# Encoder trunk on one core: expert weights stored one block per ring unit, recurrence products in halved columns, first turn started on half of the keys and values

## What is computed

```python
def wkv_scan(r, w, k, v, a, b, reverse):            # both directions, 16 heads
    def step(state, inp):
        r_t, w_t, k_t, v_t, a_t, b_t = inp
        sa = jnp.einsum('bhvk,bhk->bhv', state, a_t)
        state = state * w_t[:, :, None, :] + sa[..., None] * b_t[:, :, None, :] + v_t[..., None] * k_t[:, :, None, :]
        return state, jnp.einsum('bhvk,bhk->bhv', state, r_t)

def moe_swiglu(h, router, w13, w2):                  # 8 experts, hidden width 3584
    for e in range(N_EXPERTS):
        out = out + combine[:, e:e + 1] * swiglu(t, w13[e], w2[e])
```

## Time and profile before

| | us |
|---|---|
| median of 3 runs (2158.40 to 2160.73) | 2159.16 |
| profiled execution, its own time | 2160.95 |
| its span | 2159.1 |

### The profile page before, as it was taken

The page is one execution under the profiler, slowest core; times in us unless marked ns, Lnnn a source line. Parts: engine busy times, 40 slices in busy tenths (PEclk is TensorE's granted clock), DMA queues, the critical chain, the costliest instruction groups (busy, mean ns, idle before and its releaser), DMA issues.

```text
span 2159.1 us, 56930 instructions
## 1 busy us (share of the span) xinstructions
PE 1936.5 (90%) x26300; PEld 1585.1 (73%) x26300; DVE 511.1 (24%) x1305; ACT 261.7 (12%) x558; POOL 192.5 (9%) x318
## 2 busy tenths in 40 slices
PE   8999988999979899999789888988888888888887
PEld 4454455877635588888588887888888888888876
DVE  2132131000171546552411112011120111201200
ACT  2121121000002244332000000000000000000000
POOL 1111111000011336421000000000000000000000
PEclk9999999999989899999899999999999999999999
DMA  9432433545321011002799999999999999999992
GB/s 360 150 123 79 155 117 122 170 156 164 123 78 35 8 21 26 18 12 100 233 355 347 354 335 303 350 349 346 348 302 345 347 346 338 348 330 328 342 330 86
DMA packets 352750, 473.86 MB, mean 219 GB/s; under 512 B 30104, under 2 KB 288432, under 8 KB 352512
## 3 DMA queue, kind: packets, MB, share of 16 engines
q1 hardware_dynamic: 349632, 460.05, 63.3%
q0 software_dynamic: 2080, 7.37, 1.0%
q10 hardware_dynamic: 800, 2.76, 0.3%
HBM read 460.04 MB, written 10.10 MB: 218 GB/s over the span
## 4 chain that ended last, share of the span: by engine, by line
PE 85%; issue 7%; DVE 5%; ACT 2%; DMA 1%; POOL 1%; SPq 0%; DVEq 0%; POOLq 0%
PE ps L692 29%; PE ps L1270 14%; PE ps L683 14%; PE ps L806 12%; PE ps L744 7%; PE ps L757 3%; PE ps L860 1%; PE ps L967 1%; PE ps L773 1%; DVE arena L1874 1%; PE ps L1200 1%; DVE arena L1876 1%; PE ps L1207 0%; PE ps L791 0%; DMA arena<-wqkv 0%
## 5 line engine op out<-in xcount | busy, mean ns | idle before, releaser
L692 PE MATMUL ps<-arena 128*64 128x96 f32 x14336 | 636.5, 247 | 87.0 <-issue 86.1
L692 PEld LDWEIGHTS ps<-arena 128*64 128x64 f32 x14336 | 611.5, 137 | 107.0 <-issue 106.9
L683 PE MATMUL ps<-arena 128*128 128x128 f32 (+11 forms) x2498 | 382.4, 327 | 34.5 <-DVE arena L1861 8.3
L683 PEld LDWEIGHTS ps<-arena 128*128 128x128 f32 (+3 forms) x2498 | 297.5, 191 | 116.1 <-issue 59.2
L1270 PE MATMUL ps<-arena 128*64 128x96 f32 x7168 | 320.4, 245 | 51.7 <-issue 51.7
L1270 PEld LDWEIGHTS ps<-arena 128*64 128x64 f32 x7168 | 305.3, 136 | 61.5 <-issue 61.5
L806 PE MATMUL ps<-arena 128*128 128x512 f32 x576 | 253.4, 596 | 1.9 <-DMA arena<-wqkv 1.9
L2137 DVE TENSOR_TENSOR arena<-arena,ps 128x192 f32<-128x192 f32 x112 | 39.7, 355 | 788.9 <-ACT arena L1567 788.8
L806 PEld LDWEIGHTS ps<-arena 128*128 128x128 f32 x576 | 108.1, 191 | 128.7 <-issue 125.9
L744 PE MATMUL ps<-arena 128*128 128x256 f32 x704 | 153.8, 381 | 0.0
L744 PEld LDWEIGHTS ps<-arena 128*128 128x128 f32 x704 | 134.5, 191 | 20.2 <-issue 1.9
(11 more groups left out here) (246 smaller groups left out, 979.9 us busy)
## 6 DMA issues: line engine op xcount, KB each, us to landing
arena<-mw SPq DMA_DIRECT2D x336, 1024.0 KB, 7.9
arena<-wqkv SPq DMA_DIRECT2D x36, 1024.0 KB, 7.4
arena<-fw SPq DMA_DIRECT2D x32, 1024.0 KB, 6.4
arena<-wrkv SPq DMA_DIRECT2D x12, 1024.0 KB, 7.3
arena<-awo SPq DMA_DIRECT2D x4, 1024.0 KB, 6.2
arena<-bwo SPq DMA_DIRECT2D x4, 1024.0 KB, 11.9
xg<-arena POOLq DMA_DIRECT2D x8, 384.0 KB, 9.2
arena<-xg SPq DMA_DIRECT2D x7, 384.0 KB, 10.3
```

Source lines behind the costliest of these rows:

```text
L683: last = mm(o, a, b, start=(n == 0), stop=(n == len(pairs) - 1))
L692: last = mm(o[c], a[:, c], b, start=(n == 0), stop=(n == len(pairs) - 1))
```

## The change

Four parts.

1. The host stores w13 and w2 so that each unit is one block [128 partitions, 4096 floats]; a new `tiled_unit` loads it as two DMAs, each taking 8 KB from each of 128 rows of 16 KB. What lies in the ring slot is the same as before.
2. `add_y`, the products of `values`, and the 64-wide steps of the chain with all rows (z1 to z4 of the early half) are done in two 64-column halves, as the experts' are.
3. The first turn: DVE and POOL wait for copy 6 of `rkv_sb` in place of 8, with later waits where the other half is read (turn 2 for k, copy 10 or 12 for v); project(8) and (9) move behind the operands and systems; `inverse_rows(0, 1, 16)` and `inverse_out(0)` come before all four `pairings_out(0, i)`.
4. In the other turns inverse rows 14 and 15 and `inverse_out` move behind the copy of y and two `pairings_out`. POOL starts d_b only when the first mix is done.

```diff
             def expert_unit(item, i):
                 e, kind, n, u = item
-                w13 = mw13[bass.ds(i * 2 + e, 1)].rearrange("e (k p) n -> p (e k) n", p=P)
-                wd = mw2[bass.ds(i * 2 + e, 1)].rearrange("e (k p) n -> p (e k) n", p=P)
-                c = n * 256
-                if kind == "up":
-                    ff_unit(kind, u, (w13[:, :, c:c + 256], w13[:, :, FFE + c:FFE + c + 256]), None, FFE)
-                else:
-                    ff_unit(kind, u, None, wd[:, 4 * n:4 * n + 4, :], FFE)
+                tiled_unit(u, (mw13 if kind == "up" else mw2)[bass.ds(i * 2 + e, 1), n])
+            def tiled_unit(u, w):
+                w, half = w.rearrange("o p n -> p (o n)"), SLOT // 2
+                halves(u, (unit(u)[:, 0:half], unit(u)[:, half:]), (w[:, 0:half], w[:, half:]))
...
             def add_y(t, h, lhsT, rhs, first=False, last=False):
-                c = t * RQ + h * RH
-                return mm(ps[:, 4, c:c + RH], lhsT, rhs, start=first, stop=last, skip_group_check=True)
+                at = t * RQ + h * RH
+                for c in COLS:
+                    ins = mm(ps[c, 4, at:at + RH], lhsT[:, c], rhs, start=first, stop=last, skip_group_check=True)
+                return ins
...
-                    last = run(ps[:, 7, c:c + RH], [(gm23[i % 2][0][:, h, :], value(q, t, h))])
+                    last = by_halves(ps[:, 7, c:c + RH], [(gm23[i % 2][0][:, h, :], value(q, t, h))])
...
-                        last = run(ps[rows, bank, h * width:(h + 1) * width], [(of[:, h, rows], by[:, h, :])])
+                        o = ps[rows, bank, h * width:(h + 1) * width]
+                        product = by_halves if width == RH and rows == slice(0, P) else run
+                        last = product(o, [(of[:, h, rows], by[:, h, :])])
...
             project(7)
-            project(8)
-            project(9)
             operands(0, 0)
             operands(0, 1)
             system(0, 0)
             system(0, 1)
-            project(10)
+            project(8)
             operands(0, 2)
             operands(0, 3)
             system(0, 2)
             system(0, 3)
+            project(9)
+            project(10)
             project(11)
...
-            dve.wait_ge(rkv_sb, 8)
+            dve.wait_ge(rkv_sb, 6)
...
                 if nq:
-                    inverse_rows(nq, 11, BLK)
-                    inverse_out(nq)
+                    inverse_rows(nq, 11, 14)
                 dve.wait_ge(Y.ps, q + 1)
                 dve.wait_ge(head_done, q + 1)
                 dve.tensor_copy(y_sum.rearrange("p t n -> p (t n)"), ps[:, 4, :]).then_inc(Y.sb, 1)
                 if nq:
-                    for i in range(4):
-                        pairings_out(nq, i)
+                    pairings_out(nq, 0)
+                    pairings_out(nq, 1)
+                    inverse_rows(nq, 14, BLK)
+                    inverse_out(nq)
+                    pairings_out(nq, 2)
+                    pairings_out(nq, 3)
...
-            pairings_out(0, 0)
-            pairings_out(0, 1)
-            inverse_rows(0, 1, 7)
-            pairings_out(0, 2)
-            inverse_rows(0, 7, 12)
-            pairings_out(0, 3)
-            inverse_rows(0, 12, BLK)
+            inverse_rows(0, 1, BLK)
             inverse_out(0)
+            for i in range(4):
+                pairings_out(0, i)
...
             pool.wait_ge(rms_h, H_DONE[2])
+            pool.wait_ge(mix_ready, KB)
             pool.tensor_tensor(d_b[:, :, 0:S - 1], hR[:, :, 1:S], hR[:, :, 0:S - 1], ALU.subtract).then_inc(db_ready, 1)
...
-            pool.wait_ge(rkv_sb, 8)
+            pool.wait_ge(rkv_sb, 6)
...
+                if q == 2:
+                    pool.wait_ge(rkv_sb, 8)
...
-                if q == 0:
-                    pool.wait_ge(rkv_sb, 12)
+                pool.wait_ge(rkv_sb, 10 + 2 * (q // 2))
...
+        "mw13": a["m_w13"][0].reshape(EXPERTS, KB, P, 2, GE, 256).transpose(0, 4, 2, 1, 3, 5).reshape(EXPERTS, GE, P, SLOT),
+        "mw2": a["m_w2"][0].reshape(EXPERTS, GE // 2, 4, P, D).transpose(0, 1, 3, 2, 4).reshape(EXPERTS, GE // 2, P, SLOT),
```

More of the change, by code:

```diff
@@ L656, in _ @@
                     e = sp.value_load(over_i[0:1, bass.ds(j + (OVER + 1), 1)], min_val=0, max_val=EXPERTS - 1)
-                    w13 = mw13[bass.ds(e, 1)].rearrange("e (k p) n -> p (e k) n", p=P)
-                    wd = mw2[bass.ds(e, 1)].rearrange("e (k p) n -> p (e k) n", p=P)
                     sp.wait_ge(down_ps, j * (GE // 2) + EXPERTS * GE // 2)
@@ L665, in _ @@
                             sp.wait_ge(s, j * per + (EXPERTS * per + c))
[L666 to L670, removed]
+                        tiled_unit(u, (mw13 if kind == "up" else mw2)[bass.ds(e, 1), n])
             sp.wait_ge(experts_done, 1)
@@ L1531, in _ @@
             project_out(7)
-            project_out(8)
-            project_out(9)
             for i in (0, 1):
@@ L1537, in _ @@
                 system_out(0, i)
-            project_out(10)
+            project_out(8)
             for i in (2, 3):
@@ L1542, in _ @@
                 system_out(0, i)
-            project_out(11)
+            for c in (9, 10, 11):
+                project_out(c)
             late_keys(0, 0)
@@ L1810, in key_rates @@
                         dve.wait_ge(bonus_ok, q)
+                        dve.wait_ge(rkv_sb, 12)
                 dve.wait_ge(za.sb, q * 4 + 2 * d + 2)
@@ L2415 @@
         "g2": a["b_g2"][0], "bwo": a["b_wo"][0], "fw13": a["f_w13"][0], "fw2": a["f_w2"][0],
-        "router": a["m_router"][0], "mw13": a["m_w13"][0], "mw2": a["m_w2"][0],
+        "router": a["m_router"][0],
+        "mw13": a["m_w13"][0].reshape(EXPERTS, KB, P, 2, GE, 256).transpose(0, 4, 2, 1, 3, 5).reshape(EXPERTS, GE, P, SLOT),
+        "mw2": a["m_w2"][0].reshape(EXPERTS, GE // 2, 4, P, D).transpose(0, 1, 3, 2, 4).reshape(EXPERTS, GE // 2, P, SLOT),
     }
```

## The result

The changed kernel takes 2098.92 us (median of 4, 2084.22 to 2105.03), the kernel before 2158.78 beside it. The ratio is 0.971 (95% interval 0.966 to 0.977): 60 us faster, where 183 were forecast. Its profiled execution took 2093.34, with a span of 2091.4.

The account below looks back on a forecast made before the run. Instruction refills queued behind weight transfers were taken to bound the experts. From the profiled 2160.95 us, 137 for the experts and 46 for the recurrence came off: 1978, or 1976 as a median, range 1946 to 2014 (chance 0.58).

Parts of the forecast that it names:

- Bounds: Experts: PE's gaps are instruction refills queued behind weights until the unit in front drains; some 0.95 us a unit, gapless unit 5.36.
- Layout, the rate: Experts' weight loads: 8 KB runs move a unit in 5.05 us, the 4 KB runs' rate, against 5.71 on the mix.
- Layout, "if all of it comes off a gap": Experts: a refill waits 0.66 us less; if all comes off the 0.95 us gap, the period falls from 6.31 to about 5.65.
- queues that run empty: Experts: shorter transfers empty the queue once a unit, more refills wait only 1.6 us; period taken as 5.5, 5.36 if all do.
- Phase: Experts: part 2's 5.5 added instruction blocks move cuts half a unit, near a unit's start; most positions there give 5.4 to 5.6.
- the opposite: Experts, rival (c), slower: refills line up right behind the unit just issued, 7.2 us a unit, experts 1152, time 2193; chance 0.10.
- Rival (a): Experts: transfers gain only half as much, or refills stay in mid-load; period 6.0, experts 1018, time 2059; chance 0.17.
- Halved products: Recurrence: 64-column halves save 1.9 (early chain), 0.8 (early sums) and 3.1 us (values, add_y) a turn; last turn 4.3.
- End of a turn: Recurrence: the 2.77 us stall for masked pairings goes, 5.8 with the halved values; GT late costs 0.5 us a turn.
- First turn: Recurrence, first turn: pairings start at about 727.5 in place of 735.55, chain about 15 us later; 19 gained, bounds 11 and 21.
- "issue" below 25 us: Sign in the experts: L692's idle time released by "issue", 86.1 us before, would fall below 25.
- the first q8 packet at 1.6 us: Sign in the experts: the first instruction-refill packet after a gap comes at 1.6 us, not 4.5.

Follow-up runs that it names:

- tiny_loads: Changed kernel; from the third expert on each of a unit's two DMAs brings 64 of 2048 elements a row; sixth expert: PE busy for all of 110.9 us.
- layout_only: Kernel before with the new weight layout alone, cuts staying in mid-unit: 2120.88 us, ratio 0.981, experts 1028.2 us against 1072.0.
- pad32_7of8: Changed kernel plus 32 tiny products, weight DMAs bringing 1792 of 2048 elements from the third expert on: experts 3 to 8 749.9 us, against 763.5 with full transfers.
- first_turn_only: Kernel before with part 3 (the first turn) alone: first copy of y at 798.1 us against 816.4, experts start at 1055.2 against 1070.6.

## Why the prediction was wrong

Two steps of the sum for the experts failed: that all of the saved transfer comes off a gap, and that the move of the cuts does no harm. The recurrence came out at the forecast total, in part by luck.

**Bounds (right, with one size wrong).** Gaps are refills behind weights: shown by `tiny_loads`. A gapless unit was taken as 5.36 us; with hardly any weights it is 5.28. But a refill doesn't wait until the unit in front has drained: about 1.4 of its 2.1 MB pass first.

**Layout, the rate (right).** Up units reach the rate of the 4 KB runs. 6.03 and 5.08 came from good windows: by the share of q1 from 1100 to 1900 us, a unit held the engines for 6.22 us before (267.48 MB at 99.2%) and 5.55 after (263.45 MB at 87.2%). Both are half a microsecond longer than I took, but the difference is the 0.66 of the sum. Queue q1 in that window, before and after:

```profile
q1 hardware_dynamic: 199091, 267.48, 99.2%
...
q1 hardware_dynamic: 36525, 263.45, 87.2%
```

**Layout, "if all of it comes off a gap" (the first step that failed).** The layout gave, at one position, 44, 30 and 59 us over 168 units: 0.26, 0.18 and 0.35 us a unit (0.21, 0.21 and 0.37 by the medians), about half of the 0.66 or less. I had all of it, and another 0.15 on top for queues that run empty. Nor did the waits shrink by it: from the kernel before to `layout_only` the median wait of a refill goes from 3.8 to 3.6 us only, while the gaps become fewer (154 to 112) and shorter (1.01 to 0.77 us in the median). My explanation, not shown by a run of its own: the wait is the end of the traffic in front less the time of the request, and when the period shrinks, the next unit is issued earlier too, so that a part of what the transfer saves is taken back. It agrees in sign with `pad32_7of8`.

**Phase (seen, and taken on the wrong side: the second step that failed).** The move by half a unit was right to the record. I wrote that most positions near a unit's start give 5.4 to 5.6 and one side the opposite, and gave the opposite 0.10. The changed kernel landed on that opposite side for six of its eight experts: 1050 where the new layout in mid-unit has 1028 and 1019. My price for it, 1152, was far too high: a gap is 1 us a unit, and not one long block in two, because the refill waits for about as long as in mid-unit (medians 4.0 us, and 3.8 in the kernel before). And the good positions, -1 to -32, lie 24 records away and give 964 to 977; the forecast's 935 was reached nowhere with all weights moving. Position was the term that decided, worth 86 us against 44 for the layout. It ought to have been a case with a chance for each side, worked out from where SP's issue stands to the cut, and not part of the sum.

**Rival (a)** named half of the transfer's gain, 1018 us for the experts: it is near what the new layout gives in mid-unit (1028, 1019). For the changed kernel it is 32 too few. The Trainium skill (Runtime: NRT & Kernel Launch, Instruction fetch mechanics) calls the crossing of a block "mostly hidden". That holds where hardly any weights move (110.8 us of PE in 110.8) and for 60 us of the changed kernel's seventh expert, and fails by about 1 us a block elsewhere. The rule of the Trainium skill that a DMA engine turns between its rings packet by packet (DMA: Bandwidth & Descriptors, Queues, rings and completion order) is not tested by these runs: a packet there is a group of descriptors (about 9 to 17), while a packet of the profile is one run of up to 8 KB here (263.45 MB in 36525 packets after the change). Ahead of a refill pass 11 of the profile's packets on each of the 16 engines after the change and 74 before it (medians), and 1.4 MB in both. So the forecast's sentence that the rule would have a refill wait for one packet, against 4.5 us, compared two different things.

**Halved products (each turn within 3 us of its size).** By halves alone a turn was to give 5.8 and its last 4.3. They gave 4.5, 5.1 and 7.3. Together 17.0, or 17.8 with turn 0, of some 21.7.

**End of a turn (right alone, wrong together).** Alone, the move takes PE's stall for the first masks from 2.77 to 0.4 us, at each of three turns, and the first two periods fall by 2.3 and 3.9 us. In the last one PE waits 1.92 us for GT at 966.83, which the forecast had named as what comes next, and the copies of y are 2.5 further apart. By the start of the experts it is 4.8 us in all, where 6.6 to 8.1 were expected. Together with the halves the stall was to go, and it doesn't. PE is then faster than DVE's masks and waits 0.85, 2.19 and 0.33 us at each turn. The 2.19 stand behind the second set of values, since the mask that they wait for now comes after inverse rows 14 and 15. Waits of PE from 742 to 970 us, in the kernel before and then in the changed one (us, times, longest), and one of the stalls:

```profile
PE ps L683 <- DVE arena L1861: 8.3, 3, 2.8
...
PE ps L676 <- DVE arena L1858: 9.2, 6, 2.2
...
PE ps L676 <- DMA arena<-td: 1.0, 1, 1.0
...
796.27 1.58 PE L676 MATMUL ps<-arena 64*128 64x128 f32 x16 [2.19 <-DVE arena L1858]
```

GT came late once, by 1.0 us in all; three times 0.5 was forecast.

**First turn (its start small, the clock left out).** The pairings were forecast for 727.5 and began at 725.4. Turn 0 ended 28.9 us earlier, where 19 for its start and 8 for the turn itself make 27. The forecast has no term for the clock here. In the kernel before, the granted clock is at the lower of its two levels, 1.2 GHz, for 6.9 us from the end of PE's wait of 3.64 us on the earlier trace rows, and for 13.6 us after a wait of 2.50 us for a mask. In the changed kernel PE waits at these two places for 0.3 us or less, and the clock stays at the upper level, 2.4 GHz, from 610.5 to 924.3 us. At half the pace those 20.5 us can have cost up to 10, an estimate; how much of the 28.9 it is was not separated. Windows of the kernel before, then of the changed one:

```profile
751.30:764.90 13.60, 11.74 (x39) 9.77 (x39) 6.75 (x13) 4.33 (x7) 2.47 (x2) 0.50 0.20 41
...
610.50:924.30 313.80, 296.92 (x2792) 223.18 (x2791) 198.40 (x382) 111.40 (x222) 120.11 (x151) 1.00 0.09 20
```

The total of the recurrence, 45.8 against 46, is therefore partly luck: turns that gave less (5.8 and 7.4 in place of 8) and a start that gave more.

What would have shown it: the forecast asked for "issue" below 25 us and found 88.4, and for the first q8 packet at 1.6 us. The test was right; the weight I gave its failure was not.

## What to carry to other kernels

When an engine runs long straight code beside a saturated DMA queue, look for gaps at a fixed count of instructions and not at a tile's border, and find what was issued just ahead of the refill. Then an edit that adds code ahead of such a stage, even one that shortens its own, shifts the cuts and can cost or give more than it does itself: judge an edit by the windows of its own stage, and try a few paddings, or issue loads a quarter of a unit later, before judging the total. Don't book a shorter transfer in full: here about half of it or less came off the stage.

## What the runs showed of the hardware that was not expected

A short stall of PE can be followed by a much longer stretch at the lower clock, and for how long differs from one execution to the next. In `layout_only`, whose recurrence is that of the kernel before, the third period took 84.7 us in place of 71.6: 13 us lost behind the same 2.77 us wait for the masked pairings as in the earlier trace rows. The granted clock was at the lower of its two levels, 1.2 GHz, from 890.6 to 921.3 us, although PE was busy for all of these 30.7 us. In the kernel before it was there for only 3.4 us after that wait, and not at all after the same wait one turn earlier (2.77 us, up to 817.86); in `first_turn_only` it was there for 6.8 us after a wait of 2.76. Window 889 to 922 of `layout_only`, and of the kernel before:

```profile
889.00:922.00 33.00, 32.14 (x146) 28.07 (x147) 11.52 (x19) 5.59 (x11) 15.46 (x24) 0.53 0.09 21
...
889.00:922.00 33.00, 33.00 (x257) 30.36 (x255) 17.32 (x27) 14.51 (x31) 22.62 (x31) 0.97 0.08 17
```

0.53 of the full clock and 146 matmuls, against 0.97 and 257. The changed kernel's longest wait there is 2.2 us. The long stretch was seen in one execution and not repeated, and what decides its length is open.
